# Paged keys and values: indirect loads of four tokens to a partition from Pool, weights moved to the sync queue

## The chip, the cores and the metric

The kernel runs on one core of one Trainium2 chip. The metric is the device time of one execution in microseconds (us), as the median of several runs. All arithmetic is float32.

## The reference, cut to what matters

One decoder layer handles 256 prompt tokens and 8 sample tokens (one for each of 8 sequences with 2048 past tokens). Sample attention is the part the change touches:

```python
past_k = cache_sb_k[layer][page_table].reshape(8, 16 * 128, 8, 64)   # 16 pages of 128 tokens a sequence
z = einsum(q, k) / 8 + bias                      # stick-breaking scores, no softmax
log_rest = log_sigmoid(-z)
log_stick = cumsum(log_rest, reverse=True) - log_rest    # over all later keys
a = exp(log_sigmoid(z) + log_stick);  out = einsum(a, v)
```

Around it stand: six modulation vectors from `w_ada`, one q/k/v projection, the same stick-breaking attention and a dilated softmax attention for the prompt, dilated attention of the samples over a 2048-token window (whose cache is also an output, shifted by one token), an output projection, and a PEER layer: top-16 of 16384 experts for each token and head, whose rows of 8 KB are gathered and weighted.

## The kernel before, in words

Each engine has its own program, and semaphores order them. All 48 weight chunks of 1 MB (line 378, a round is 4 chunks) are loaded by Pool's queue into four slots `R[0..3]`: rounds 0 and 1 are modulation, 2 to 4 q/k/v, 5 to 8 modulation again, 9 output projection, 10 and 11 the expert queries. A chunk's load waits until the tensor engine has used the one four before it (`w_used`).

The sync engine (SP) loads small inputs, then the K pages (line 285), each a direct DMA of 256 KB whose page number it reads into a register. A chunk is two pages (tokens on the partitions) in one of four slots; 64 chunks make up K, and 64 make up V. It waits for `k_used` or `v_used` of the chunk four before. SP also issues the copies of the window caches to the outputs (line 296): 64 pieces of 1 MB from HBM to HBM, in `copy_piece`. A piece waits for the landing of the previous piece on its own of four semaphores, so up to four are in flight. The order on SP is: 24 pieces early, then all K chunks, ten stores of new keys and values (lines 322 and 324), V chunks with some pieces between, the DV windows, and the remaining pieces.

VectorE (DVE) multiplies every K chunk by the query (line 1140) and reduces it over each head (line 1142), in `page_scores`. Sequences 0 to 3 are handled beside the q/k/v projection. Sequences 4 to 7 are threaded into four rounds of prompt attention, `sticks_pair(g)` on TensorE (PE): DVE's part of such a round is, in order, a scale (L1158), two chunks, L1164 and L1166, two chunks, L1170, two chunks, L1174, two chunks, a copy (L1177). PE computes two modulation chunks (L472) before and two after its own matmul in the round.

Pool applies the rotary factors (L395 to L399) once q/k/v is ready, stores two rows (L402, L403) and goes on with the weights. When K is done, DVE, ScalarE (ACT) and PE turn the scores into sticks: DVE sums over later pages in 15 steps (L1240), PE does the sum over tokens (L649, L650), DVE subtracts (L1246). Then `dilated_pair` on PE alternates V matmuls (`pages_pv`, L594: one matmul a page, in halves of 8 pages) with dilated prompt attention. Pool meanwhile fetches windows of the dilated K cache (L261, L262), which DVE consumes (L1221, L1223). After that come DV windows (L699), the output projection and queries (L510, L744), and the expert stream: Pool gathers 1 MB per slot by indirect DMA (L432), DVE dots it (L1454), PE accumulates (L791).

Of the kernel before, what the change touches and what calls it, by code (L numbers as in the profile page):

```python
# [35 lines left out]
KVP = 2  # L36
KVS = 4
CPB = NPG // KVP
# [20 lines left out]
for _name, _n in (("ident", P), ("tri", P), ("ones", P), ("later", P), ("cnt", 384), ("dbias", 384),  # L59
                  ("scnt", 384), ("sbias", 384), ("rope", 48), ("hmask", DG), ("unit8", 64), ("rep8", P), ("fold8", NB), ("iota", TOPK)):  # L60
    _CONST[_name] = (_at, _n)
    _at += _n
# [3 lines left out]
def constants():  # L66
# [36 lines left out]
    put("fold8", np.tile(np.eye(NB, dtype=np.float32), (2 * NH, 1)))  # L103
    put("iota", np.tile(np.arange(TOPK, dtype=np.float32), (P, 1)))
# [20 lines left out]
def build(nc, A):  # L125
    ctx = ExitStack()
    with ctx:
# [9 lines left out]
        def cst(name):  # L137
# [15 lines left out]
        zrow = sb("zrow", [NB * NH, 384])  # L153
# [5 lines left out]
        pages = sb("pages", [1, NB * NPG], I32)  # L159
# [12 lines left out]
        diag = sb("diag", [P, 4, P])  # L172

# [3 lines left out]
        KV = [Rf[:, WSLOTS * 2048 + s * 1024:WSLOTS * 2048 + (s + 1) * 1024].rearrange("p (g n) -> p g n", g=KVP)  # L177
              for s in range(KVS)]

# [6 lines left out]
        z1, zt, zl = Z[:, 0, :], Z[:, 1, :], Z[:, 2, :]  # L186

# [16 lines left out]
        def row_slot(k):  # L204
# [25 lines left out]
          kst dst sbs dis tks subk_in z_v topsm tope fin_in""".split()  # L230
# [36 lines left out]
        def _(sp):  # L267
# [12 lines left out]
            def page_chunk(b, c, cache, ready, waits):  # L280
                for sm, v in waits:
                    sp.wait_ge(sm, v)
                for g in range(KVP):
                    page = sp.value_load(pages[0:1, bass.ds(b * NPG + c * KVP + g, 1)], min_val=0, max_val=cache.shape[0] - 1)  # L284
                    sp.dma_start(KV[c % KVS][:, g, :],  # L285
                                 cache[bass.ds(page, 1)].rearrange("a p n -> (a p) n")).then_inc(ready[c % KVS], 16)
# [20 lines left out]
            for c in range(CPB):  # L307
                page_chunk(0, c, A["sb_k"], k_ready, [(s["k_used"], c - KVS + 1)] if c >= KVS else [])
                if c == KVS - 1:
                    copy_windows(0, 0)  # L310
                    copy_windows(0, 1)
                    copy_windows(1, 0)

            with sp.Fori(1, NB) as b:
                for c in range(CPB):
                    page_chunk(b, c, A["sb_k"], k_ready, [(s["k_used"], b * CPB + (c - KVS + 1))])


# [7 lines left out]
            def value_pages(b, first=False, q=None):  # L326
                for c in range(CPB):
                    page_chunk(b, c, A["sb_v"], v_ready,
                               [] if first and c < KVS else [(s["v_used"], b * CPB + (c - KVS + 1))])
                    if q is not None and c % 4 == 1:  # L330
                        copy_piece(2, 0, c // 4, q)


            for m in range(2):
                copy_piece(1, 1, m, 0)
            sp.wait_ge(s["k_used"], NB * CPB)
            value_pages(0, first=True, q=0)
            with sp.Fori(1, NB // 2) as i:
                value_pages(i * 2 - 1)
                value_pages(i * 2, q=i)  # L340
            value_pages(NB - 1)

# [26 lines left out]
        def _(pool):  # L369
            for k in range(WSLOTS):  # L370
                pool.dma_start(R[:, k, :], A["wts"][k]).then_inc(w_ready[k], 16)

            def weight_rounds(first, end):
                with pool.Fori(first, end) as r:
                    for k in range(WSLOTS):

                        pool.wait_ge(s["w_used"], r * WSLOTS + (k - WSLOTS + 1))
                        pool.dma_start(R[:, k, :], A["wts"][bass.ds(r * WSLOTS + k, 1)].rearrange("a p n -> (a p) n")  # L378
                                       ).then_inc(w_ready[k], 16)

            weight_rounds(1, 6)
# [22 lines left out]
            weight_rounds(6, 9)  # L404
# [6 lines left out]
            weight_rounds(9, 10)  # L411
            with pool.Fori(1, NB // 2) as i:
                for j in range(2):
                    pool.wait_ge(s["dk_used"], i * 2 + (j - 1))
                    window_rows(pool, DK, i * 2 + j, j, A["dil_k"], A["dil_k_s"], dk_ready)
# [1132 lines left out]
```

## Time and profile before

| | before |
|---|---|
| median of 3 runs | 1369.17 us (1368.55 to 1369.77) |
| profiled execution, first to last instruction | 1367.5 us |
| TensorE busy | 1121.9 us, 82% |
| VectorE busy | 790.2 us, 58% |
| ScalarE busy | 374.5 us, 27% |
| GpSimd busy | 389.7 us, 28% |
| moved by DMA | 479.79 MB, mean 351 GB/s |
| DMA queue of Pool | 332.47 MB |
| DMA queue of SP | 146.92 MB |

The profile gives no separate end-to-end time for its own execution; its span is 1.7 us below the median of the timed runs. Busy times overlap each other, so the shares say which engine could bound a stage, and only the order of the waits in that stage says which one does.

### The profile page before, as it was taken

The numbers are of one execution on the slowest core, as the hardware profiler recorded it, in microseconds if no ns is written. First come the engines' busy times: TensorE is split into PE (matmuls) and PEld (weight loads), VectorE is DVE, ScalarE is ACT, GpSimd is POOL, SyncE is SP. The second block draws the span as 40 slices with busy tenths as digits, with TensorE's granted clock in tenths as the row PEclk, the third lists the DMA queues.
The fourth block names the chain that finished last, engine by engine and source line by source line (L and its number), as shares of the span: only waits on it lengthen the run. The fifth ranks groups of instructions, "written<-read, shape, count | busy, mean of one in ns | idle before, by whom it ended". The sixth has DMA issues, their size and how long they took to land.

```text
span 1367.5 us, 14726 instructions
## 1 busy us (share of the span) xinstructions
PE 1121.9 (82%) x3386; PEld 503.3 (37%) x3386; DVE 790.2 (58%) x1679; ACT 374.5 (27%) x1030; POOL 389.7 (28%) x384
## 2 busy tenths in 40 slices
PE   6799998998787888998997778777768777777875
PEld 2375774443221211457852323233223333232321
DVE  4203996976512411324437777777777677777755
ACT  1201004434110000002233333333344334444323
POOL 1000003020201000000125555555535555555540
PEclk9898999996999997998999999999999999999998
DMA  9998887898698886899659999999999999999995
GB/s 335 426 358 303 298 312 270 323 356 301 220 284 252 251 269 215 322 390 339 232 207 423 422 422 422 422 422 422 422 421 379 422 422 422 422 422 422 422 422 221
DMA packets 91422, 479.79 MB, mean 351 GB/s; under 512 B 11792, under 2 KB 11817, under 8 KB 50172
## 3 DMA queue, kind: packets, MB, share of 16 engines
q0 software_dynamic: 46912, 332.47, 60.3%
q1 hardware_dynamic: 44476, 146.92, 30.9%
q8 instruction: 15, 0.25, 0.1%
q14 instruction: 19, 0.16, 0.0%
HBM read 476.10 MB, written 70.32 MB: 400 GB/s over the span
## 4 chain that ended last, share of the span: by engine, by line
PE 37%; DMA 32%; issue 10%; DVE 8%; SPq 6%; ACT 4%; POOL 2%; POOLq 0%; DVEq 0%; ACTq 0%
DMA R<-in_uv,idst 26%; PE ps L510 13%; PE ps L791 8%; PE ps L744 4%; SPq L284 3%; DMA R<-in_sb_v 3%; PE ps L472 3%; SPq L285 2%; DVE R L1140 2%; PE ps L699 2%; PE ps L594 2%; POOL R L432 2%; DMA R<-in_sb_k 2%; PE ps L481 1%; ACT wgt L1050 1%
## 5 line engine op out<-in xcount | busy, mean ns | idle before, releaser
L791 PE MATMUL ps<-R,diag 128*128 128x512 f32 x1024 | 482.1, 619 | 153.4 <-ACT diag L1069 153.4
L432 POOL DMA_INDIRECT R<-in_uv,idst x256 | 320.9, 1254 | 332.5 <-PE ps L791 260.4
L1454 DVE CUSTOM_DVE_ANT_0 R<-R,H 128x1024 f32<-128x1024 f32 x264 | 318.6, 1222 | 162.7 <-DMA R<-in_uv,idst 152.3
L791 PEld LDWEIGHTS ps<-R,diag 128*128 128x128 f32 x1024 | 192.4, 196 | 443.1 <-ACT diag L1069 241.6
L510 PE MATMUL ps<-R,HT 128*128 128x256 f32 (+1 forms) x768 | 172.7, 384 | 1.0 <-DVE HT L1335 0.4
L378 POOL DMA_DIRECT2D R<-in_wts x44 | 23.4, 531 | 508.9 <-PE ps L510 341.9
L594 PE MATMUL ps<-R,ast 128*8 128x512 f32 x256 | 123.0, 625 | 27.6 <-DMA R<-in_sb_v 24.0
L510 PEld LDWEIGHTS ps<-R,HT 128*128 128x128 f32 (+1 forms) x768 | 119.0, 158 | 55.3 <-issue 12.1
L1047 ACT ACTIVATE gel<-dots 128x2 f32<-128x2 f32 x132 | 26.8, 203 | 377.3 <-DVE dots L1454 377.3
L1140 DVE TENSOR_TENSOR R<-R 128x1024 f32<-128x1024 f32 x64 | 78.2, 1221 | 66.2 <-ACT R L874 57.6
L472 PE MATMUL ps<-R,cT 128*9 128x256 f32 x384 | 92.8, 398 | 1.3 <-ACT bsel L821 1.3
L1069 ACT ACTIVATE diag<-const,wgt 128x128 f32<-128x128 f32 x256 | 89.1, 394 | 16.1 <-PE ps L791 3.2
L1142 DVE TENSOR_REDUCE Z<-R 128x1024 f32 x64 | 78.1, 1220 | 9.1 <-DVE R L1140 0.2
L1258 DVE TENSOR_TENSOR msk<-ps,const 8x512 f32<-8x512 f32 x16 | 10.9, 679 | 97.4 <-PE ps L594 57.5
L594 PEld LDWEIGHTS ps<-R,ast 128*8 128x8 f32 x256 | 20.8, 92 | 119.6 <-issue 67.9
L1050 ACT ACTIVATE wgt<-gel,gst 128x1 f32<-128x1 f32 x264 | 63.3, 287 | 4.3
L744 PE MATMUL ps<-HT,R 128*128 128x264 f32 x256 | 59.9, 393 | 0.3 <-ACT HT L855 0.3
L472 PEld LDWEIGHTS ps<-R,cT 128*9 128x9 f32 x384 | 34.3, 94 | 55.8 <-issue 14.8
L744 PEld LDWEIGHTS ps<-HT,R 128*128 128x128 f32 x256 | 49.0, 194 | 8.6 <-ACT HT L855 0.4
L863 ACT ACTIVATE QKV<-ps 128x512 f32 (+1 forms) x12 | 7.2, 598 | 120.9 <-PE ps L510 120.9
L261 POOL DMA_DIRECT2D m_all<-in_dil_k x24 | 12.9, 538 | 95.6 <-DVE zd L1223 95.0
L699 PE MATMUL ps<-R,ast 128*8 128x512 f32 (+2 forms) x48 | 29.8, 775 | 7.9 <-DMA R<-out_dil_v_s 5.8
(233 smaller groups left out, 872.3 us busy)
## 6 DMA issues: line engine op xcount, KB each, us to landing
R<-in_wts POOLq DMA_DIRECT2D x48, 1024.0 KB, 8.1
R<-in_sb_k SPq DMA_DIRECT2D x128, 256.0 KB, 4.4
R<-in_sb_v SPq DMA_DIRECT2D x128, 256.0 KB, 3.4
out_dil_k_s<-in_dil_k SPq DMA_DIRECT2D x32, 1023.5 KB, 8.0
out_dil_v_s<-in_dil_v SPq DMA_DIRECT2D x32, 1023.5 KB, 7.9
R<-in_uv,idst POOLq DMA_INDIRECT x256, 12.1
m_all<-in_dil_k POOLq DMA_DIRECT2D x16, 192.0 KB, 6.1
R<-in_dil_v SPq DMA_DIRECT2D x16, 192.0 KB
```

The lines of the kernel that those rows point to most:

```text
L432: pool.indirect_dma_start(out=R[:, row_slot(k), :], out_offset=None, in_=A["uv"], in_offset=bass.IndirectOffsetOnAxis(ap=idst[:, par, k:k ...
L472: last = pe.matmul(out, cT[:, c, :], W[k][:, c, :], start=(c == 0), stop=False)
L510: last = pe.matmul(out, hT[:, c, t * P:t * P + TP[t]], W[k][:, c, :], start=(c == 0), stop=(c == KC - 1))
L594: last = pe.matmul(ps[0:NH, 6 + j, :], ast[:, j, c * KVP + g, :], KV[c % KVS][:, g, :], start=(c + g == 0), stop=(c * KVP + g == NPG - 1))
L699: last = pe.matmul(ps[0:NH, 6 + j, :], ast[0:n, j, g, :], DV[j][0:n, g, :], start=(g == 0), stop=(g == 2))
L744: last = pe.matmul(ps[:, j, 0:NTOK], W[k][:, c, j * P:(j + 1) * P], hT[:, c, :], start=(c == 0), stop=(c == KC - 1))
L791: last = pe.matmul(ps[:, banks + q, :], diag[:, k % 4, :], R[:, row_slot(k), D + q * 512:D + (q + 1) * 512], start=False, stop=False, skip ...
L1050: last = act.activation(wgt[:, k + q:k + q + 1], gel[:, k + q:k + q + 1], ACT.Copy, scale=gst[:, k + q:k + q + 1])
L1069: act.activation(diag[:, k % 4, :], ident, ACT.Copy, scale=wgt[:, k:k + 1]).then_inc(s["diag_done"], 1)
L1140: kc.inc(dve.tensor_tensor(kv, kv, q, ALU.mult))
L1142: dve.tensor_reduce(z4[:, c * KVP:(c + 1) * KVP, bass.ds(b, 1), :].rearrange("p g a h -> p g (a h)"), kv.rearrange("p g (h d) -> p g h d", ...
L1454: dve.tensor_tensor_reduce(u, u, H[:, t, :], 1.0, 0.0, ALU.mult, ALU.add, dots[:, k:k + 1]).then_inc(s["dot_done"], 1)
```

## The change

K and V pages are read through one view of the cache in which a row is 4 tokens (8 KB). A chunk is now four pages (1 MB): each partition gets four consecutive tokens of one page, 32 partitions to a page. There are 32 K and 32 V chunks, in two slots of 1 MB in place of four of 0.5 MB. Row numbers are computed once by DVE from the page table. Pool issues the chunks, one indirect DMA each, in program order with rotary work and windows. The weights move to SP, each followed by a copy piece in rounds 1 to 4 and 6 to 8. The sum over later keys is regrouped to fit the new token order.

```diff
-KVP = 2
-KVS = 4
-CPB = NPG // KVP
+QUAD = 32
+QUADS = P // QUAD
+KVT = P // QUAD
+KVS = 2
+CPB = NPG // KVT
+KVN = NB * CPB
@@ sync
-            sp.dma_start(pages[:, :], A["pages"]).then_inc(s["small_in"], 16)
-            sp.wait_ge(s["small_in"], 64)
+            for q in range(QUADS):
+                sp.dma_start(pages[q * QUAD:(q + 1) * QUAD, :], A["pages"][q:q + 1].to_broadcast([QUAD, KVN])).then_inc(s["pages_in"], 16)
+            for k in range(WSLOTS):
+                sp.dma_start(R[:, k, :], A["wts"][k]).then_inc(w_ready[k], 16)
+            def weight(r, k):
+                sp.wait_ge(s["w_used"], r * WSLOTS + (k - WSLOTS + 1))
+                sp.dma_start(R[:, k, :], A["wts"][bass.ds(r * WSLOTS + k, 1)].rearrange("a p n -> (a p) n")
+                             ).then_inc(w_ready[k], 16)
...
+            for k in range(WSLOTS):
+                weight(1, k)
+                copy_piece(0, k // 2, k % 2, 0)
+            with sp.Fori(2, 5) as r:
+                for k in range(WSLOTS):
+                    weight(r, k)
+                    copy_piece(0, k // 2, k % 2, r - 1)
+            for k in range(WSLOTS):
+                weight(5, k)
             sp.wait_ge(s["rot_done"], 6)
...
+            for k in range(WSLOTS):
+                copy_piece(1, k // 2, k % 2, 0)
+            with sp.Fori(6, 9) as r:
+                for k in range(WSLOTS):
+                    weight(r, k)
+                    copy_piece(1, k // 2, k % 2, r - 5)
+            for k in range(WSLOTS):
+                weight(9, k)
+            for q in range(4):
+                for k in range(WSLOTS):
+                    copy_piece(2, k // 2, k % 2, q)
             sp.wait_ge(s["new_out"], 32)
             sp.wait_ge(s["dk_used"], NB)
...
-                    copy_piece(1, 1, j, i)
-            sp.wait_ge(s["v_used"], NB * CPB)
+                    copy_piece(3, 0, j, i - 1)
+            sp.wait_ge(s["v_used"], KVN)
             sp.dma_start(subk, A["subk"].rearrange("p (g n) -> p g n", g=16)).then_inc(s["subk_in"], 16)
-            for pair, odd in ((2, 1), (3, 0), (3, 1)):
-                copy_windows(pair, odd)
+            with sp.Fori(10, 12) as r:
+                for k in range(WSLOTS):
+                    weight(r, k)
+            for m in range(2):
+                copy_piece(3, 0, m, 3)
+            copy_windows(3, 1)
@@ gpsimd
+            def page_rows(n, cache, ready, used):
+                if used is not None:
+                    pool.wait_ge(*used)
+                pool.indirect_dma_start(
+                    out=R[:, WSLOTS + n % KVS, :], out_offset=None, in_=cache,
+                    in_offset=bass.IndirectOffsetOnAxis(ap=pages[:, n:n + 1], axis=0),
+                ).then_inc(ready[n % KVS], 16)
+            pool.wait_ge(s["rows_ready"], 1)
+            for n in range(KVN // 2):
+                page_rows(n, A["sb_k"], k_ready, (s["k_used"], n - KVS + 1) if n >= KVS else None)
             pool.wait_ge(s["qkv_ev"], QKV_CH)
...
-            weight_rounds(6, 9)
+            for n in range(KVN // 2, KVN):
+                page_rows(n, A["sb_k"], k_ready, (s["k_used"], n - KVS + 1))
...
+            for i in range(NB // 2):
+                for n in range(i * 2 * CPB, (i + 1) * 2 * CPB):
+                    page_rows(n, A["sb_v"], v_ready, (s["v_used"], n - KVS + 1) if n >= KVS else (s["k_used"], KVN))
+                    if i < NB // 2 - 1 and n % CPB == 1:
+                        w = n // CPB + 2
+                        pool.wait_ge(s["dk_used"], w - 1)
+                        window_rows(pool, DK, w, w % 2, A["dil_k"], A["dil_k_s"], dk_ready)
@@ tensor
-            for half in range(2):
-                c = slice(half * 512, (half + 1) * 512)
-                pe.matmul(ps[:, 3 + half, :], tri, zl[:, c], start=True, stop=False)
-                last = pe.matmul(ps[:, 3 + half, :], ones, zt[:, c], start=False, stop=True)
+            n = CPB * PAIRS
+            pe.matmul(ps[:, 3, 0:n], tri, zt[:, 2 * n:3 * n], start=True, stop=False)
+            pe.matmul(ps[:, 3, 0:n], ones, zt[:, 3 * n:4 * n], start=False, stop=True).then_inc(s["z_s"], 1)
@@ vector: row numbers, page_scores on 128x2048 instead of 128x1024, the suffix sum
+            step(dve.tensor_scalar(rows_f[:, :], rows_f[:, :], float(QUAD), cst("place"), ALU.mult, ALU.add))
...
-                page_scores(g + 4, (0, 1))
+                page_scores(g + 4, (0,))
...
-            for g in range(NPG - 2, -1, -1):
+            step(dve.tensor_tensor(two, L[:, :, 0, :], L[:, :, 1, :], ALU.add))
+            step(dve.tensor_tensor(three, two, L[:, :, 2, :], ALU.add))
+            step(dve.tensor_tensor(total, three, L[:, :, 3, :], ALU.add))
```

## Rows read from the trace of the kernel before

**Rows 1.** Windows: stretch, its length, busy us by engine, PEclk, DMA share, GB/s.
```profile
0.00:123.50 123.50, 102.00 (x395) 53.54 (x396) 22.64 (x20) 21.20 (x48) 8.86 (x20) 0.90 0.96 370
123.50:215.40 91.90, 88.96 (x401) 61.03 (x400) 76.78 (x66) 9.90 (x22) 8.46 (x18) 0.98 0.85 286
215.40:320.00 104.60, 92.72 (x441) 44.91 (x441) 93.29 (x96) 37.85 (x70) 19.23 (x34) 0.89 0.91 326
346.40:512.80 166.40, 140.42 (x363) 30.52 (x363) 50.80 (x100) 14.29 (x39) 12.65 (x24) 0.95 0.84 262
560.00:705.80 145.80, 137.64 (x624) 102.28 (x624) 59.48 (x165) 27.85 (x82) 12.34 (x17) 0.94 0.80 296
705.80:1367.00 661.20, 497.02 (x1055) 194.72 (x1053) 466.81 (x1182) 245.35 (x729) 328.13 (x271) 0.97 0.98 408
```

**Rows 2.** DVE timeline, 123 to 323 us: start, duration, instruction, idle before it.
```profile
123.52 1.22 DVE L1140 TENSOR_TENSOR R<-R 128x1024 f32<-128x1024 f32 x1 [57.60 <-ACT R L874]
124.88 1.22 DVE L1142 TENSOR_REDUCE Z<-R 128x1024 f32 x1
126.01 1.22 DVE L1140 TENSOR_TENSOR R<-R 128x1024 f32<-128x1024 f32 x1
...
204.59 1.22 DVE L1142 TENSOR_REDUCE Z<-R 128x1024 f32 x1
214.35 1.14 DVE L1158 TENSOR_SCALAR H<-ps,sbb 128x384 f32<-128x384 f32 x2 [8.54 <-PE ps L554]
215.41 1.21 DVE L1140 TENSOR_TENSOR R<-R 128x1024 f32<-128x1024 f32 x1
...
240.48 1.13 DVE L1158 TENSOR_SCALAR H<-ps,sbb 128x384 f32<-128x384 f32 x2
...
289.63 1.14 DVE L1158 TENSOR_SCALAR H<-ps,sbb 128x384 f32<-128x384 f32 x2
...
319.95 1.22 DVE L1230 SCALAR_TENSOR_TENSOR Z<-Z,sbb 128x1024 f32<-128x1024 f32 x1
```

**Rows 3.** Waits, 215 to 320 us: DVE's on K pages.
```profile
DVE R L1140 <- DMA R<-in_sb_k: 6.5, 4, 3.2
```

**Rows 4.** POOL timeline, 210 to 223 us.
```profile
210.96 1.69 POOL L395 TENSOR_TENSOR Z<-QKV,const 128x128 f32<-128x128 f32 x4
...
221.32 0.59 POOL L402 DMA_DIRECT2D out_dil_k_s<-QKV  x1 [0.29 <-POOL QKV L399]
221.90 0.51 POOL L403 DMA_DIRECT2D out_dil_v_s<-QKV  x1
```

**Rows 5.** SP timeline: first and last of the ten stores.
```profile
310.78 1.24 SPq L322 DMA_DIRECT2D out_sb_k_p<-QKV  x2
...
317.33 0.97 SPq L324 DMA_DIRECT2D out_sb_v_n<-QKV  x1
```

**Rows 6.** DMA issues at 676, 189, 79, 587 and 635 us, last column us to landing.
```profile
R<-in_uv,idst POOLq DMA_INDIRECT x1, 5.6
...
R<-in_wts POOLq DMA_DIRECT2D x1, 1024.0 KB, 6.0
...
R<-in_wts POOLq DMA_DIRECT2D x1, 1024.0 KB, 13.3
...
R<-in_wts POOLq DMA_DIRECT2D x1, 1024.0 KB, 15.8
...
R<-in_wts POOLq DMA_DIRECT2D x1, 1024.0 KB, 10.8
```

**Rows 7.** PE timeline, 337 to 513 us.
```profile
337.50 1.92 PE L649 MATMUL ps<-Z,const 128*128 128x512 f32 x2
...
342.02 1.02 PE L650 MATMUL ps<-Z,const 128*128 128x512 f32 x2
...
346.36 7.03 PE L594 MATMUL ps<-R,ast 128*8 128x512 f32 x16 [1.59 <-ACT HT L887]
...
512.79 1.98 PE L481 MATMUL ps<-m_rows,const 9*128 9x512 f32 x4
```

**Rows 8.** Waits, 345 to 515 us: PE's on V pages and on ACT.
```profile
PE ps L594 <- DMA R<-in_sb_v: 24.0, 21, 3.6
PE ps L594 <- ACT HT L887: 3.4, 3, 1.6
```

**Rows 9.** SP timeline: the last copy piece.
```profile
643.30 0.51 SPq L296 DMA_DIRECT2D out_dil_v_s<-in_dil_v  x1
```

**Rows 10.** Timeline: Pool's first four weight loads, PE's first use of one.
```profile
1.41 2.32 POOL L371 DMA_DIRECT2D R<-in_wts  x4 [0.84 <-POOLq L1540]
...
14.13 5.09 PE L472 MATMUL ps<-R,cT 128*9 128x256 f32 x16 [0.60 <-ACT bsel L821]
```

More of the change, by code:

```diff
@@ L103, in constants @@
     put("fold8", np.tile(np.eye(NB, dtype=np.float32), (2 * NH, 1)))
+    put("place", (np.arange(P) % QUAD)[:, None].astype(np.float32))
     put("iota", np.tile(np.arange(TOPK, dtype=np.float32), (P, 1)))
@@ L158, in build @@
         gcol = sb("gcol", [P, KC])
-        pages = sb("pages", [1, NB * NPG], I32)
+        pages = sb("pages", [P, KVN], I32)
+        rows_f = sb("rows_f", [P, KVN])
         stat = sb("stat", [P, 32])
@@ L176, in build @@
         W = [R[:, s, :].rearrange("p (c n) -> p c n", c=KC) for s in range(WSLOTS)]
-        KV = [Rf[:, WSLOTS * 2048 + s * 1024:WSLOTS * 2048 + (s + 1) * 1024].rearrange("p (g n) -> p g n", g=KVP)
-              for s in range(KVS)]
+        KV = [R[:, WSLOTS + s, :].rearrange("p (g n) -> p g n", g=KVT) for s in range(KVS)]
         m_flat = m_all[:, :, :].rearrange("p s n -> p (s n)")
@@ L324, in _ @@
                 sp.dma_start(A[name], QKV[0:NB, 2, col:col + DG]).then_inc(s["kv_out"], 16)
[L326 to L341, printed above, removed]
+            for k in range(WSLOTS):
[9 more added lines that the diff above has]
+                    copy_piece(2, k // 2, k % 2, q)
             sp.wait_ge(s["new_out"], 32)
@@ L369, in _ @@
         def _(pool):
[L370 to L381, printed above, removed]
+            def page_rows(n, cache, ready, used):
[8 more added lines that the diff above has]
+                page_rows(n, A["sb_k"], k_ready, (s["k_used"], n - KVS + 1) if n >= KVS else None)
             pool.wait_ge(s["qkv_ev"], QKV_CH)
@@ L410, in _ @@
                 window_rows(pool, DK, b, b, A["dil_k"], A["dil_k_s"], dk_ready)
[L411 to L415, printed above, removed]
-            weight_rounds(10, CHUNKS // WSLOTS)
+            for i in range(NB // 2):
[5 more added lines that the diff above has]
+                        window_rows(pool, DK, w, w % 2, A["dil_k"], A["dil_k_s"], dk_ready)
             def head_rows(i, par, first):
@@ L590, in pages_pv @@
                     pe.wait_ge(s["ast_ready"], i + 1)
-                for c in range(half * 4, half * 4 + 4):
-                    pe.wait_ge(v_ready[c % KVS], (i * 2 + (c // KVS + 1)) * 32)
-                    for g in range(KVP):
-                        last = pe.matmul(ps[0:NH, 6 + j, :], ast[:, j, c * KVP + g, :], KV[c % KVS][:, g, :],
-                                         start=(c + g == 0), stop=(c * KVP + g == NPG - 1))
+                for c in range(half * 2, half * 2 + 2):
+                    pe.wait_ge(v_ready[c % KVS], (i * 2 + (c // KVS + 1)) * 16)
+                    for g in range(KVT):
+                        last = pe.matmul(ps[0:NH, 6 + j, :], ast[:, j, c * KVT + g, :], KV[c % KVS][:, g, :],
+                                         start=(c + g == 0), stop=(c * KVT + g == NPG - 1))
                     last.then_inc(s["v_used"], 1)
@@ L1117, in modulate @@
                     dve.tensor_tensor(H[0:n, t, :], H[0:n, t, :], b, ALU.add).then_inc(s["h_ready"], 1)
+            dve.wait_ge(s["pages_in"], 16 * QUADS)
+            dve.wait_ge(s["c_in"], 48)
+            step(dve.tensor_copy(rows_f[:, :], pages[:, :]))
+            step(dve.tensor_scalar(rows_f[:, :], rows_f[:, :], float(QUAD), cst("place"), ALU.mult, ALU.add))
+            dve.tensor_copy(pages[:, :], rows_f[:, :]).then_inc(s["rows_ready"], 1)
             dve.memset(m_all[:, 0:2, :], 0.0)
```

71 lines of the change are left out of this document (31 added, 40 removed).

## The prediction

> **What bounds the kernel now.** I read the windows by stage first, then the timeline of each engine in the stages that the change touches, then the waits there and the landing times of single DMAs. The windows [rows 1] give six stages. Up to 123.5 us and again from 560 to 705.8 us PE is the engine that runs through. From 123.5 to 215.4 us PE is busy 89.0 of 91.9 us with the q/k/v projection, and DVE does the first half of K beside it: its last reduce starts at 204.59 and it then idles 8.5 us for PE [rows 2]. From 215.4 to 320 us DVE is busy 93.3 of 104.6 us: this stage is DVE's. From 346.4 to 512.8 us PE is busy 140.4 of 166.4 us and waits 24.0 us for V pages [rows 1, 8]. From 705.8 us DMA moves 408 GB/s at a share of 0.98: the expert stream is bound by DMA, the change does not touch it, and it shifts as a whole with whatever comes before. So the change is decided between 123 and 513 us.
>
> The sums below are against the profiled execution, whose span is 1367.5 us; the median of the runs is 1.7 us above it, and I add the sum to the median.
>
> **The latency that decides: F.** With two slots of 1 MB, a chunk's load can start only when the chunk two before it is used. Call F the time from that point to usable data. A gather of the same shape (128 rows of 8 KB, from Pool) that ran alone landed 5.6 us after its issue [rows 6]; with 0.2 us for the wake-up F is 5.8. A Pool load of the same size beside SP's smaller page loads took 6.0. But Pool loads that ran while SP had up to four copy pieces in flight landed after 13.3, 15.8 and 10.8 us [rows 6]. The bounds are therefore 5.8 and 15.8. In the first four rounds of K after the change, SP's queue holds weights and copies in turn for most of the time, and I take F = 11 there, nearest to the lowest of the three contended rows because SP's queue also runs dry between its waits on `w_used`.
>
> By the Trainium skill (DMA: Bandwidth & Descriptors, Queues, rings and completion order) each DMA engine takes turns between the queues that have work, a packet at a time. By that rule the time would be that of the faster rival's upper end, 1364 us, and by the rows it is the sum below. The rows of 10.8 to 15.8 us do not agree with even turns.
>
> **First half of K (123.5 to 215.4).** A pair of 0.5 MB chunks costs 2 x (126.01 - 123.52) = 4.98 us of DVE now [rows 2]. One instruction over 2048 elements instead of two over 1024 saves its start: the gap of 1.36 us to the reduce and 1.13 us to the next chunk hold about 0.36 us that isn't proportional in all, so I take 4.6 us for 1 MB. Both slots are filled long before. Then two chunks cost F + 4.6. SP issues one weight and one piece in every 10.7 us here, which is about half the load of the contended rows: F about 8, between 5.8 and 11. Fourteen chunks after the first two: 7 x (8 + 4.6) + 9.2 = 97 us, so DVE ends near 221 instead of 206. DVE isn't needed before 215.4, and what follows waits for something later anyway (next step), so I cost it at nothing. If F were 11 this half would end at 242 and add some 8 us; that is kept for the range.
>
> **Chunk 16 comes late.** Now SP has the fifth sequence's chunks in place and DVE starts on them at 215.41. After the change the seventeenth chunk is behind Pool's rotary work in program order: that runs from 210.96 and its two stores end at 222.4 [rows 4]. The chunk is issued at 222.6 and is there at 233.6. At the same moment SP, released by the same rotary work, puts out ten stores (7.5 us of issuing [rows 5], 2.1 MB) and four copy pieces.
>
> **Second half of K (215.4 to 320).** Per round DVE has, beside four chunks, about 4.6 us of its own work in between (1.6, 0.9, 0.7 and 1.4). First round at F = 11: chunk 16 from 234 to 238.6, chunk 17 from 240.3 to 244.9, chunk 18 (issued 238.8) from 249.8 to 254.4, chunk 19 (issued 245.1) from 256.1 to 260.7, next round at 261.1. Before it was 240.48 [rows 2]: +20.6 us. Second and third round have four weights and four pieces each on SP: 2 x (11 + 4.6) = 31.2 us a round, against (289.63 - 240.48) / 2 = 24.6 [rows 2]: +13.2. In the fourth round SP has only the four weights of the output projection, F about 7.5: 24.2 us against 30.3 (in which 5.6 of the 6.5 us of DVE's waits for K now lie [rows 3]): -6.1. The end of K moves by 20.6 + 13.2 - 6.1 = +27.7 us. At F = 5.8 throughout, the same count gives 250.4 for the first round, then 23.1 us a round, bound by DVE: K ends at 319.7, +-0. At F = 15.8 it is +60.
>
> **Sticks (320 to 346.4).** The 15 adds are replaced by a shorter chain, but PE gets to the triangular product only at 337.5, long after they end, so they are worth nothing. The product takes 337.50 to 343.04 [rows 7] for eight records of 512 columns; four of 256 columns should take a quarter: -4 us. Bounds 0 and -5.5.
>
> **V (346.4 to 512.8).** Four chunks of 0.5 MB take PE 7.03 us [rows 7], so 1 MB takes 3.5. A half of `pages_pv` is two new chunks; there are 16 halves, 10.4 us each today. After the change each takes the larger of 7.03 + what PE has in between (about 1.3) and F + 3.5 = 9.3 at F = 5.8. SP's 16 pieces of the third pair start about 10 us before K ends and need at least 16.8 MB / 0.4 = 42 us, so they reach some 10 us into V: one half at 11 + 3.5 = 14.5. The first half has its data already (8.4), fourteen take 9.3, and the 3.4 us of waits on ACT stay [rows 8]: 8.4 + 130.2 + 14.5 + 3.4 = 156.5 against 166.4: -10 us. At F = 11 for six halves it would be +16; with no wait at all, 136 us, -30. Pool's window loads (2.2 us each) stand behind a V chunk and before the next trigger, which comes 3.5 us or more later, so they are hidden, except the first, which waits for DVE: within the 14.5.
>
> **The rest.** The first weights are issued by SP behind the small loads, near 8 us instead of 1.41; PE starts on them at 14.13 us [rows 10], when 2.6 MB of small loads and the first weight have passed at 370 GB/s [rows 1]: nothing, at most +2. The last ten pieces now wait behind the last weight at about 660 us, where before the last was issued at 643.30 [rows 9]. They share 10.5 MB with the first eight gathers; 18.9 MB fit into the 46 us to 705.8 at 408 GB/s, barely: +1.5 us, between 0 and +6. PE's weights for the second round of the K stage lie behind the stores and four pieces: 7.3 MB from 223 us, at the 290 GB/s which SP has when Pool takes a share, land at 248, and PE wants them at 261. They are covered by DVE's own lateness; without that lateness they would cost up to 8 us.
>
> **Sum.** +27.7 - 4 - 10 + 1.5 = +15.2 us; 1369.2 + 15.2 = 1384.4, rounded to 1385 us.
>
> **The rivals.**
> *Faster: K is not held up by SP's queue.* One mechanism: Pool's megabyte gets at least an even share. At the 408 GB/s of the expert stream 1 MB takes 2.6 us, so another megabyte beside it makes F = 5.8 + 2.6 = 8.4, and F is between 5.8 and that. For it: rows with SP's page loads in flight show 6.0; DMA has room, a share of 0.85 before 215 us [rows 1]. Against it: the rows of 13.3 and 15.8 [rows 6], and that 12 MB a round over the 23.1 us of DVE work would be 545 GB/s, above the 408 of the expert stream. At 8.4 K ends +10 (first round at 255, two of 26, one of 23.4), V -12, sticks -4, tail +1: 1364. At 5.8: 0 - 4 - 15 = 1350. The middle is 1357. The sign turns near F = 9. Chance 0.30.
> *No change.* F near 9, both cancel: 1367 to 1372. Chance 0.08.
> *PE starves for weights.* SP, one program, waits for a piece to land before it may issue the next weight; with Pool's queue busy, pieces land after 15 us and PE waits 8 us in each of three rounds on top of the forecast: 1385 + 24 = 1409. For it: weight and piece alternate on one queue; against: PE needs a weight only some 20 us after its slot comes free. Chance 0.09.
> *The page load is no better for being in rows of 8 KB*, F is above 11 in V too: +16 instead of -10 in V, so 1411. Only bandwidth sharing could do this and the copies end early. Chance 0.03.
>
> **How the numbers follow.** The forecast, F near 11 where SP's queue is full, has 0.50: 1385 us, with its own range 1374 to 1402. What a measurement of this kernel can tell from no change is 0.2%, 2.7 us. Faster 0.30; same 0.08; slower 0.50 + 0.09 + 0.03 = 0.62. The range that leaves out 2 in 10 runs from 1352, near the low end of the faster rival, to 1406.
>
> **What would show it.** Right: in the changed profile the first page product of the second half of K starts at 230 us or later instead of 215.4, after Pool's rotary work; single K loads between 222 and 300 us land after 9 us or more; DVE's waits for K grow from 6.5 to over 25 us in that stage; in V the halves are 9.3 us apart and PE's wait for V persists. Wrong: K loads landing in under 8 us beside SP's copies; PE waiting for weights on the critical chain; V longer than 166 us; or the expert stream changing its own length of 661 us by more than 3.

## The result and the profile after

| | before | after |
|---|---|---|
| median of 4 runs | 1369.47 us (1368.55 to 1374.68) | 1441.81 us (1438.16 to 1448.38) |
| ratio to before, 95% interval | | 1.0524 (1.0489 to 1.0559) |
| span of the profiled execution | 1367.5 us | 1446.6 us |
| first page product of K's second half | 215.41 | 236.78 |
| end of K (first L1230, now L1243) | 319.95 | 367.73 |
| PE ready for V; end of V | 346.4; 512.8 | 388.8; 593.2 |

The change makes the kernel 5.2% slower: the direction was forecast, but the size was 72 us instead of 16, outside the range. The spans differ by 79.1 us (the profiled execution of after was the longest of its four, at 1448.38 us). By stage that is +47.8 to the end of K, -5.3 in the sticks (21.1 against 26.4 us), +38.0 in V (204.4 against 166.4) and -1.4 in the rest.

Windows by stage of after, with the columns of [rows 1]:

```profile
0.00:125.40 125.40, 103.14 (x395) 54.87 (x396) 23.27 (x24) 21.24 (x48) 2.24 (x6) 0.90 0.68 273
125.40:226.40 101.00, 95.38 (x431) 63.05 (x429) 72.93 (x33) 9.92 (x22) 31.42 (x31) 0.99 0.72 270
226.40:367.70 141.30, 93.59 (x412) 47.70 (x412) 90.57 (x65) 38.33 (x70) 23.65 (x28) 0.76 0.95 371
388.80:593.20 204.40, 148.20 (x362) 32.43 (x362) 52.60 (x103) 15.92 (x43) 45.11 (x54) 0.87 0.70 239
640.00:783.00 143.00, 134.69 (x607) 99.83 (x606) 54.57 (x153) 28.08 (x83) 8.68 (x10) 0.95 0.50 185
783.00:1446.00 663.00, 505.19 (x1052) 198.17 (x1050) 470.14 (x1190) 245.77 (x729) 327.62 (x270) 0.95 0.98 409
```

DVE does no more work in the third row than before (90.6 against 93.3 us, [rows 1]); the row is 37 us longer because DVE waits. DMA's share was 0.85 in K's first half and is 0.72 now, and from 640 to 783 us it is 0.50, where in the matching stage before it was 0.80. So there was room for the copies, but not where SP now puts them.

DVE timeline of after, answering [rows 2] (start, duration, instruction, idle before it):

```profile
125.36 2.29 DVE L1153 TENSOR_TENSOR R<-R 128x2048 f32<-128x2048 f32 x1 [59.26 <-ACT R L881]
...
226.35 1.13 DVE L1171 TENSOR_SCALAR H<-ps,sbb 128x384 f32<-128x384 f32 x2
236.78 2.29 DVE L1153 TENSOR_TENSOR R<-R 128x2048 f32<-128x2048 f32 x1 [9.30 <-DMA R<-in_sb_k,pages]
...
259.12 2.29 DVE L1153 TENSOR_TENSOR R<-R 128x2048 f32<-128x2048 f32 x1 [10.05 <-DMA R<-in_sb_k,pages]
...
270.84 1.13 DVE L1171 TENSOR_SCALAR H<-ps,sbb 128x384 f32<-128x384 f32 x2
...
367.73 1.28 DVE L1243 SCALAR_TENSOR_TENSOR Z<-Z,sbb 128x1024 f32<-128x1024 f32 x1
```

POOL timeline of after, answering [rows 4]: the rotary work starts 6 us later than before, because a page load stands ahead of it, and chunk 16 stands behind it.

```profile
213.89 2.93 POOL L381 DMA_INDIRECT R<-in_sb_k,pages  x1 [4.76 <-DVE Z L1155]
216.93 1.69 POOL L402 TENSOR_TENSOR Z<-QKV,const 128x128 f32<-128x128 f32 x4
...
228.74 1.02 POOL L381 DMA_INDIRECT R<-in_sb_k,pages  x1 [0.30 <-issue]
```

Waits of after: DVE's on K pages from 226 to 368 us (6.5 us in [rows 3]), then PE's on V pages from 388 to 595 us (24.0 us in [rows 8]).

```profile
DVE R L1153 <- DMA R<-in_sb_k,pages: 47.5, 11, 10.1
...
PE ps L603 <- DMA R<-in_sb_v,pages: 56.1, 18, 12.9
```

PE timeline of after, answering [rows 7]. The triangular product is over at 387.1. The second V record below is one chunk, 8 matmuls, 18 us after the first.

```profile
385.37 1.06 PE L657 MATMUL ps<-Z,const 128*128 128x256 f32 x2
386.22 0.84 PE L658 MATMUL ps<-Z,const 128*128 128x256 f32 x2
...
396.91 5.29 PE L603 MATMUL ps<-R,ast 128*8 128x512 f32 x8 [8.12 <-DMA R<-in_sb_v,pages]
415.06 6.46 PE L603 MATMUL ps<-R,ast 128*8 128x512 f32 x8 [12.86 <-DMA R<-in_sb_v,pages]
...
433.30 2.73 PE L603 MATMUL ps<-R,ast 128*8 128x512 f32 x3 [10.91 <-DMA R<-in_sb_v,pages]
```

DMA issues of after at 242.2, 248.4, 367.8, 369.1 and 402.5 us, answering [rows 6] (last column: us to landing). All five are beyond my upper bound of 15.8.

```profile
R<-in_sb_k,pages POOLq DMA_INDIRECT x1, 16.9
...
R<-in_sb_k,pages POOLq DMA_INDIRECT x1, 17.4
...
R<-in_sb_v,pages POOLq DMA_INDIRECT x1, 29.0
...
R<-in_sb_v,pages POOLq DMA_INDIRECT x1, 45.9
...
R<-in_sb_v,pages POOLq DMA_INDIRECT x1, 30.8
```

SP timeline of after: the first of the ten stores and of the copies in K [rows 5], then the first and the last of the 16 pieces put out before V, and the last piece before the query weights [rows 9].

```profile
227.03 0.82 SPq L331 DMA_DIRECT2D out_sb_k_p<-QKV  x2
...
233.97 0.56 SPq L307 DMA_DIRECT2D out_dil_k_s<-in_dil_k  x1
...
363.02 0.54 SPq L307 DMA_DIRECT2D out_dil_k_s<-in_dil_k  x1
...
415.30 0.51 SPq L307 DMA_DIRECT2D out_dil_v_s<-in_dil_v  x1
...
627.31 0.54 SPq L307 DMA_DIRECT2D out_dil_v_s<-in_dil_v  x1
```

PE's first use of a weight comes at 15.79 us instead of 14.13 [rows 10].

### The profile page after: what moved, and what is told of

It reads as the page before. It is cut to its first block, busy times and chain, and to the rows that moved or that the text cites. A ratio compares the mean times of both kernels' runs of the same rounds, so it can differ in the third digit from the quotient of the medians.

```text
span 1446.6 us, 12757 instructions
## 1 busy us (share of the span) xinstructions
PE 1136.9 (79%) x3382; PEld 512.0 (35%) x3382; DVE 784.5 (54%) x1612; ACT 375.7 (26%) x1030; POOL 440.7 (30%) x400
## 4 chain that ended last, share of the span: by engine, by line
DMA 43%; PE 31%; DVE 10%; issue 8%; POOL 3%; ACT 3%; SPq 1%; POOLq 0%; DVEq 0%; ACTq 0%
DMA R<-in_uv,idst 22%; DMA R<-in_sb_k,pages 9%; DMA R<-in_sb_v,pages 9%; PE ps L798 8%; PE ps L519 6%; PE ps L603 6%; PE ps L751 4%; DVE R L1153 3%; DVE Z L1155 2%; POOL R L441 2%; PE ps L481 2%; DVE R L1473 2%; PE ps L706 1%; PE ps L490 1%; DMA R<-in_uv,idec 1%
## 5 line engine op out<-in xcount | busy, mean ns | idle before, releaser
L798 PE MATMUL ps<-R,diag 128*128 128x512 f32 x1024 | 491.4, 630 | 147.1 <-ACT diag L1076 147.1
L798 PEld LDWEIGHTS ps<-R,diag 128*128 128x128 f32 x1024 | 196.4, 199 | 442.2 <-ACT diag L1076 230.3
L603 PE MATMUL ps<-R,ast 128*8 128x512 f32 x256 | 130.4, 663 | 56.2 <-DMA R<-in_sb_v,pages 56.1
L1153 DVE TENSOR_TENSOR R<-R 128x2048 f32<-128x2048 f32 x32 | 73.4, 2294 | 132.6 <-DMA R<-in_sb_k,pages 73.2
L381 POOL DMA_INDIRECT R<-in_sb_k,pages x32 | 42.0, 1313 | 303.0 <-DVE Z L1155 287.8
L481 PE MATMUL ps<-R,cT 128*9 128x256 f32 x384 | 96.4, 409 | 2.3 <-DMA R<-in_wts 2.3
L381 POOL DMA_INDIRECT R<-in_sb_v,pages x32 | 34.0, 1064 | 152.6 <-PE ps L603 146.0
L1155 DVE TENSOR_REDUCE Z<-R 128x2048 f32 x32 | 73.2, 2286 | 5.3 <-DVE R L1153 1.5
L1277 DVE TENSOR_TENSOR msk<-ps,const 8x512 f32<-8x512 f32 x16 | 10.9, 678 | 99.2 <-PE ps L603 62.7
L1057 ACT ACTIVATE wgt<-gel,gst 128x1 f32<-128x1 f32 x264 | 63.5, 288 | 4.3
L429 POOL COPY idst<-idx 128x16 int32 (+1 forms) x16 | 7.2, 447 | 146.6 <-DVE gall L1463 146.6
```

The lines of the kernel that those rows point to most:

```text
L381: pool.indirect_dma_start(out=R[:, WSLOTS + n % KVS, :], out_offset=None, in_=cache, in_offset=bass.IndirectOffsetOnAxis(ap=pages[:, n:n + ...
L481: last = pe.matmul(out, cT[:, c, :], W[k][:, c, :], start=(c == 0), stop=False)
L603: last = pe.matmul(ps[0:NH, 6 + j, :], ast[:, j, c * KVT + g, :], KV[c % KVS][:, g, :], start=(c + g == 0), stop=(c * KVT + g == NPG - 1))
L798: last = pe.matmul(ps[:, banks + q, :], diag[:, k % 4, :], R[:, row_slot(k), D + q * 512:D + (q + 1) * 512], start=False, stop=False, skip ...
L1057: last = act.activation(wgt[:, k + q:k + q + 1], gel[:, k + q:k + q + 1], ACT.Copy, scale=gst[:, k + q:k + q + 1])
L1153: kc.inc(dve.tensor_tensor(kv, kv, q, ALU.mult))
```

## Experiments

All ratios are to the kernel before, on the same chip, with 95% intervals; medians of different kernels were in part taken on different chips, on which the kernel before took 1368.9 to 1370.3 us. The stages come from one execution of each kernel. In the diffs `pieces(n)` puts out the next n of the 64 copy pieces in their fixed order. Stages of each profile, in us (V from the start of the second triangular matmul record to the end of the last page product; waits of DVE for K pages and of PE for V pages in the whole kernel):

| kernel | K ends | V | waits K | waits V | ratio |
|---|---|---|---|---|---|
| before | 319.95 | 170.8 | 8.5 | 24.0 | 1 |
| after | 367.73 | 207.0 | 73.2 | 56.1 | 1.0524 |
| no copies | 341.35 | 171.2 | 47.2 | 27.6 | 0.9999 |
| copies out of V | 362.21 | 173.2 | 68.2 | 26.2 | 1.0285 |
| copies out of K | 338.57 | 199.3 | 44.1 | 51.3 | 1.0336 |
| both | 340.85 | 175.6 | 46.6 | 28.4 | 1.0140 |
| rotary later | 370.93 | 200.6 | 67.4 | 55.5 | 1.0547 |
| one piece in flight | 361.21 | 195.9 | 52.4 | 42.0 | 1.0516 |
| half slots, both | 329.85 | 150.0 | 25.9 | 9.7 | 0.9868 |
| half slots alone | 364.43 | 178.3 | 57.2 | 38.9 | 1.0373 |
| half slots, both, rotary later | 330.48 | 148.4 | 21.7 | 11.1 | 0.9889 |
| before, copies beside K | 343.27 | 170.2 | 32.1 | 26.1 | 1.0081 |
| both, query in PSUM | 338.26 | 167.3 | 45.0 | 23.3 | 1.0082 |

**No copies.** Theory: what costs is the copies on SP's queue beside Pool's loads.

```diff
 def pieces(n):
-    for _ in range(n): copy the next piece
+    pass
```

> All 64 copy pieces of the window caches are left out (two outputs are therefore not written except for the new row); everything else is as after the change. Theory A (Pool's page loads get a small share while SP's queue holds copy pieces): single page loads land in 5.5 to 8 us in every stage, K ends near 325 us instead of 368, V takes about 160 us instead of 204, the whole about 1355 us. Theory B (two slots and program order cost it, with or without copies): K still ends after 350 us and the whole stays above 1410 us. Theory C (indirect page loads are slow in themselves, or starved by DVE): landings stay above 9 us and the whole above 1420 us.

Measured: 1372.94 us, ratio 0.9999 (0.9971 to 1.0028). All of the loss is gone, but none of the gain that Theory A expected appears. K still ends 21.4 us later than before and V is as long as before. Some 8 us come back between the end of V and the first expert product (157 us instead of 165); the kernel before with copies beside K, which leaves no copy out, has 155 us there, so it is not shown that the spared copies save them. Windows of this kernel in K's second half and in V:

```profile
222.20:341.40 119.20, 91.90 (x437) 45.28 (x435) 90.36 (x66) 38.29 (x70) 25.71 (x34) 0.87 0.84 303
364.20:531.00 166.80, 139.17 (x363) 31.68 (x363) 51.59 (x100) 14.34 (x39) 44.84 (x54) 0.95 0.65 220
```

**Copies out of V only, and out of K only.** The 16 pieces before V go behind V in the first kernel; the 16 of K's second half go early, beside the q/k/v weights, in the second.

```diff
@@ first kernel
-            pieces(16)                       # before V
@@ after V: 4 pieces, then 2 with each of the eight last weights
@@ second kernel
-    weight(r, k); pieces(1)                  # r = 1 to 4, and 6 to 8
+    weight(r, k); pieces(1, 3, 3, 1 for r = 1 to 4), none from r = 5 on
-            pieces(4)                        # after the ten stores
```

> Only the 16 pieces that stood before V move to the stages after V. Theory A: the first two V loads land in under 9 us, not 29 and 46; V takes about 160 us; the whole drops by about 40 us, to 1400 us. Theory B: V shortens by under 10 us. In the later stages the pieces lie beside PE-bound work and cost 0 to 5 us.

Measured: 1409.96 us, ratio 1.0285 (1.0246 to 1.0325). V shrinks by 34 us, and PE's waits for V are back where they were before the change.

> Only the 16 pieces that lay beside the second half of K move ahead, before 125 us, where the copies ran in the kernel before. Theory A: K loads between 225 and 360 us land in 6 to 9 us instead of 8 to 17, K ends near 330 us, the whole drops by 35 to 40 us, to about 1405 us. Theory B: K ends no more than 12 us earlier, 1430 us.

Measured: 1415.2 us, ratio 1.0336 (1.0288 to 1.0384). K ends 29 us earlier, and V stays bad.

**Both.** Copies neither in K's second half nor before V.

> Both groups of 16 pieces are moved: 32 pieces ahead of 125 us, none beside the second half of K or beside V, the rest after V. If the two moves add up: 1442 - 32 - 27 = 1383 us. Theory A (copies in SP's queue starve Pool's page loads) then has accounted for nearly all of the loss, and K ends near 341 us as in the kernel without copies. Theory B (two slots and program order) owns what is left against 1370 us: the 21 us by which K still ends later.

Measured: 1386.52 us, ratio 1.014 (1.0096 to 1.0185). The two effects nearly add up: 2.4% and 1.9% of the 5.2%, 3.8% together. Its median is 14 us above that of the kernel without copies, while the spans of the two profiles differ by 2.8 us only. That is because the profiled execution of this kernel was the shortest of its four (1382.16 us, 4.4 below the median), and the one without copies was 6.4 above its median. So copies may still cost up to 14 us in the other stages, and the profiles don't place them.

**Rotary work behind two more page loads.** Rival to the queue: it is the program order on Pool that makes K late.

```diff
-            for n in range(KVN // 2):        # page loads ahead of the rotary work
+            for n in range(KVN // 2 + 2):
```

> Only Pool's order changes: chunks 16 and 17 of K are issued ahead of the rotary work. Theory A: DVE's 9.3 us wait for chunk 16 goes down to about 3, but the following loads meet SP's queue as before; -3 to -8 us, 1436 us. Theory B (program order is a main cause): -15 us or more.

Measured: 1448.77 us, ratio 1.0547 (1.0498 to 1.0596): no gain. The DVE timeline of this kernel shows chunk 16 on time, but the next two loads are then issued only at 244.3 and 245.6 us, behind the same rotary work: the wait for chunk 16 turns into one of 9.95 us for chunk 18.

```profile
228.09 1.13 DVE L1171 TENSOR_SCALAR H<-ps,sbb 128x384 f32<-128x384 f32 x2
229.13 2.34 DVE L1153 TENSOR_TENSOR R<-R 128x2048 f32<-128x2048 f32 x1
```

SP's stores, pieces and weights all wait for the rotary work too, so PE now runs out of weights in K's second half. PE's waits for them in the whole kernel (2.3 us in after):

```profile
PE ps L481 <- DMA R<-in_wts: 21.6, 6, 12.2
```

So this run moves the rotary work's lateness rather than removing it. It shows that two loads ahead of it gain nothing, not that the order on Pool is free.

**One piece in flight instead of four.** Is it the depth of SP's queue that holds Pool's loads up?

```diff
 def pieces(n):
     for each piece:
+        sp.wait_ge(landing of the piece before it)
         copy the piece
```

> The order of the changed kernel, but each copy piece waits for the landing of the piece issued before it, so one is in flight instead of four. If the depth of SP's queue sets Pool's share (Theory A): V loads at the start of V land in 9 to 12 us instead of 29 and 46, and V is shorter by 20 us or more, although the same bytes move beside it; the whole 1405 to 1420 us. If only the bytes count (rival): V is as long as before, 1435 us or more, and weights behind a piece come later.

Measured: 1439.12 us, ratio 1.0516 (1.046 to 1.0571). The V loads land sooner, the gain doesn't show: V is 11 us shorter, not 20. Queues of DMA in after from 376 to 415 us, beside four pieces (packets, MB, share of the engines' time):

```profile
q1 hardware_dynamic: 351, 11.46, 81.1%
q0 software_dynamic: 352, 2.22, 18.9%
```

The same of the kernel with one piece in flight, 391 to 440 us:

```profile
q1 hardware_dynamic: 239, 8.32, 45.7%
q0 software_dynamic: 1357, 8.21, 44.8%
```

With four pieces in SP's queue Pool gets 2.22 of 13.7 MB and its V loads land after 29 to 46 us; with one piece the two queues move about the same bytes and V loads land after 16 to 17 us at first, then 7.5 to 12. But SP's program now stops at each piece until the one before has landed, the weights behind it come late, and the copies beside V last until 477 us. Waits of the same kernel:

```profile
DVE R L1172 <- DMA R<-in_sb_k,pages: 52.4, 20, 10.6
PE ps L622 <- DMA R<-in_sb_v,pages: 42.0, 18, 5.2
...
PE ps L500 <- DMA R<-in_wts: 31.1, 9, 10.9
```

DVE and PE wait 35 us less for pages and PE 29 us more for weights (2.3 in after). That is my rival in which PE starves for weights; it holds in this kernel and, with 21.6 us, where the rotary work is later, but not in after.

**Four slots of 0.5 MB, copies moved.** What is left after the copies: with two slots, every second load starts only when a whole megabyte has been used. The same view in rows of two tokens (4 KB), four slots, still indirect from Pool.

```diff
-KVS = 2
+KVS = 4                                      # 0.5 MB each
-    out=R[:, WSLOTS + n % KVS, :], in_offset=rows pages[:, n]
+    out=R[:, WSLOTS + n % KVS // 2, half n % 2], in_offset=rows 2 * pages[:, n // 2] + n % 2
```

> As e7_all_pieces_moved, and each 1 MB chunk is loaded as two indirect DMAs of 0.5 MB (rows of 2 tokens, 4 KB) into four slots, each with a semaphore of its own, with 64 K and 64 V loads. Theory B (two slots are too few, since a load can't start before the chunk two before it is used): DVE waits for K drop from 47 to under 20 us, V from 166 to about 150 us, the whole to 1355 us or less, below the kernel before. Theory D (Pool issues each load late because it is held up while DVE runs on two SBUF inputs, 2.74 instead of 0.94 us): twice as many issues are held up and the whole is not better than e7.

Measured: 1353.13 us, ratio 0.9868 (0.9825 to 0.9911): 1.3% faster than the kernel before, and 2.7% faster than the same order of copies in slots of 1 MB. Windows of this kernel in K's second half and in V:

```profile
218.40:329.90 111.50, 89.11 (x429) 44.19 (x427) 93.79 (x98) 38.05 (x70) 51.62 (x50) 0.85 0.90 327
353.40:498.30 144.90, 133.36 (x362) 31.16 (x362) 51.33 (x100) 14.30 (x39) 72.44 (x84) 0.98 0.77 254
```

V is 21 us shorter than before [rows 1]; from the first round of K's second half to its end it is still 6 us longer (111.5 against 105.6).

**Four slots, copies where the change put them.**

> The half loads of e9 (four slots of 0.5 MB) with the pieces where the change put them. If depth and copies add up: 1442 - 33 = 1409 us. Theory A (starvation beside the copies in V doesn't depend on the slots): V begins late all the same, the first V loads take over 25 us, 1405 to 1420 us. Rival (half loads slip between the copies): below 1390 us.

Measured: 1419.91 us, ratio 1.0373 (1.0324 to 1.0422). It is 11 us above the 1409 of a plain sum. Half slots do not protect from the copies: the first four V loads land after 45.3 to 56.4 us. DMA queues of this kernel, 385 to 412 us:

```profile
q1 hardware_dynamic: 259, 8.52, 87.8%
q0 software_dynamic: 258, 0.94, 13.1%
```

**Four slots, copies moved, rotary work later.** The two edits above together.

> e9 with the first four loads of the second half of K issued ahead of the rotary work. In e9 DVE waits 10.5 us there. Theory (program order costs it once no copies are in the way): that wait falls to about 1 us, K ends 6 to 9 us earlier, 1345 us. Rival (the rotary work and the ten stores only move, and weights for the next round come later): within 2 us of e9, or slower.

Measured: 1353.13 us, ratio 0.9889 (0.9847 to 0.9932): the same as without the later rotary work. DVE's wait of 10.5 us at 230.0 becomes one of 8.0 us at 241.0, and K ends at 330.48 instead of 329.85. Putting the rotary work behind a few more loads gains nothing in either setting; what Pool's order costs as such stays untested.

**The kernel before, with copies beside K.** Would the old design be hurt by copies as well?

```diff
@@ kernel before, K chunks of sequences 4 to 7
+                    if c % 2:
+                        copy_piece(1, c // 4, c // 2 % 2, b - 4)
```

The same pieces leave the early batch and the V stage.

> The kernel before, with 16 pieces moved into SP's program beside the second half of K, one after every second chunk, as many as the changed kernel has there; pages still on SP, weights on Pool. Theory A in its general form (DMA is near its limit in that stage, and any copy there costs): K ends 20 to 35 us later, 1390 to 1400 us. Rival (only Pool's loads behind SP's copies suffer): K ends within 10 us, below 1380 us.

Measured: 1379.79 us, ratio 1.0081 (1.0053 to 1.0109). The whole ends between the two expectations, but K ends 23.3 us later (343.27 instead of 319.95), as Theory A in its general form has it: the same pieces cost the end of K 29.2 us in the changed kernel (367.73 - 338.57). So page loads on SP's own queue suffer from copies beside them nearly as much as Pool's do. The whole is only 10 us longer because 11 us come back between the end of V and the first expert product (155 us instead of 165). There the granted clock was 0.93 instead of 0.89 and PE was busy 144.1 instead of 151.3 us, and its waits for DV windows fell by 4.1 us; why the clock was higher is open. K pages of 256 KB take 9.4 us to land here (median, 240 to 300 us) and 4.9 in the kernel before in the same window.

**Scores with the query in PSUM.** See the last section for what it tests. Based on the kernel with both groups moved; the first four sequences' scores take another operand of the same shape.

```diff
-                    q = QB[:, b, :]          # SBUF
+                    q = ps[:, 4, :]          # PSUM, sequences 0 to 3
```

> e7 with the multiply of the first four sequences reading its second operand from PSUM in place of SBUF (the query there is not the right one, so the scores of these sequences are wrong; shapes and order are the same). Theory D (an indirect DMA on Pool is held up while DVE runs a tensor_tensor on two SBUF operands): in the first half of K all issues take 0.94 us, none 2.74; the waits of 3 us every second chunk fall to about 1.2, the first half ends 8 to 12 us earlier (near 214), the whole 3 to 8 us less than e7. Rival (2.74 us is Pool's own cost): the durations stay.

Measured: 1381.68 us, ratio 1.0082 (1.0056 to 1.0107), against 1.014 (1.0096 to 1.0185) without this edit; the intervals overlap, so a gain is not shown. The first half of K ends 2 us earlier, not 8 to 12, and the end of K 2.6 us. V differs by 8 us between the two profiles (167.3 and 175.6), though nothing in V was edited: differences of a few us between stages of single executions say little.

## Why the forecast had the right sign and the wrong size

**What held.** "Chunk 16 comes late": issued at 228.7 and first used at 236.8, forecast 222.6 and 233.6, by the mechanism named, though partly by luck: the issue was 6 us later than forecast and the landing, 7.9 us, 3 us shorter. The lone F, about: with no copies the first two V loads land after 8.2 and 9.3 us and the later ones after 5.4 to 8.6. Sticks: -5.3 against -4. The rest: -1.4 against +1.5, the expert stream 663 us against 661. The low chance of the rival in which PE starves: PE waits 2.3 us for weights in after. K loads between 222 and 300 us landed after 9.8 to 17.4 us but for the first one at 7.9, above the 9 that I named.

**The step that failed most: V, -10 forecast, +38.0 measured.** What failed is the price of the loads that meet the copies: I took F = 11 for one half and let the copies end 42 us after their start. In fact the four pieces in flight left Pool's queue 19% of the engines' time, loads landed after 29 to 46 us, and the 16 pieces were issued from 363.0 to 415.3 and so ended about 14 us (a piece's median landing) later, near 430: 67 us. PE's waits grew by 32.1 us and its busy time by 7.8 (148.2 against 140.4, at a mean clock of 0.87 against 0.95). Moving these pieces takes 34 us from V and 32 from the whole, which settles the cause. Nor was the number out of reach. I had read three contended rows; beside the early copies the trace of before holds a worse one, a weight load of Pool's issued at 49.14 us (DMA issues of the kernel before):

```profile
R<-in_wts POOLq DMA_DIRECT2D x1, 1024.0 KB, 28.0
```

(Part of it is a wait behind Pool's own previous load, which was issued at 44.33 and landed at 63.5.) A bound of 28 instead of 15.8 would have shown that the place of the pieces decides. My argument that the copies "end early" was the error: they were slow for the same reason that the pages were. The rival in which F is above 11 in V too, to which I gave 0.03, names what happened.

**The contended rows had half the depth.** I said that they ran while SP had "up to four copy pieces in flight". In the kernel before, the pieces of a window take turns on two of the four semaphores, so mostly two are in flight: 2.0 on average beside the load issued at 78.3 us, 2.4 beside the one at 587.3 and 2.0 beside the one at 634.6. The change goes round all four semaphores, so four are. That part of the change is not in my list of what it does. Landing of the pieces of one cache, before and after (last column, us):

```profile
out_dil_k_s<-in_dil_k SPq DMA_DIRECT2D x32, 1023.5 KB, 8.0
out_dil_k_s<-in_dil_k SPq DMA_DIRECT2D x32, 1023.5 KB, 14.6
```

With one piece in flight it is 7.1. No run has the change with two in flight and the pieces where it put them, so what the depth alone costs stays open: the run with one piece in flight has the late weights on top.

**K's second half, +27.7 forecast, +47.8 measured.** The forecast adds up the ends of the rounds. End of the first round: +20.6 forecast, +30.4 measured (270.84 instead of 240.48). About 3 us of the excess lie before chunk 16, which was first used at 236.78 instead of 233.6, and 6.6 after it: the next two loads, issued at 242.19 and 248.41, landed after 16.9 and 17.4 us and not after 11. Second and third rounds: +13.2 forecast, +21.1 measured (70.2 us instead of 49.2). They took 36.6 and 33.6 us, which the forecast's own 2 x (F + 4.6) gives at F = 13.7 and 12.2; single loads landed after 8.2 to 14.5 us. Fourth: -6.1 forecast, -3.7 measured (26.7 instead of 30.3). So the term that was mis-sized is again F beside the copies. The first half of K, which I put at nothing, ended at 226.4 and not at 221. DVE then still waited 9.3 us for chunk 16, so this lateness counted only by another way: Pool's rotary work is queued behind the last page load of the first half, which waits for DVE, so it moved from 210.96 to 216.93, and chunk 16 with it.

**Terms hidden under the first error.** With the copies gone K still ends 21.4 us late, where I forecast nothing at F = 5.8. Of these, 17.1 us are there at the end of the first round (257.60 instead of 240.48), after a wait of 11.6 us for chunk 16; this is the place where Pool's program order and the landing time work together, and no run takes them apart. Single loads land after 5.5 to 10.9 us even then, beside the weights on SP. Issues that DVE holds up (below) add little: without them K ends 2.6 us earlier. V without copies took 166.8 us, where the terms of the forecast at F = 5.8 give 8.4 + 15 x 9.3 + 3.4 = 151 us: its halves took 10.7 us on average (15 of them from 364.20 to 524.02), not 9.3. So about 15 of the 48 us by which V was missed are there without the copies. The same shows in after, where the halves from 539 us on took 10.4 to 12.4 us, with no copy left from that stage and no window load. Four slots take 11 us from the end of K and 26 us from V, against the same order of copies in two slots. That the slots and not the row size are the reason is likely but not isolated: rows shrank from 8 to 4 KB together with the chunks, so the runs show only that the longer rows bring nothing which outweighs the fewer slots.

**Even turns between queues.** By the Trainium skill (DMA: Bandwidth & Descriptors, Queues, rings and completion order) each engine takes turns among the queues that have work, one packet at a time. The prediction read this as even bytes, so that F is at most 8.4, and held its rows of 10.8 to 15.8 us against it. That reading was wrong. The fences above count 351 packets of SP's queue to 352 of Pool's beside four pieces, and 259 to 258 with half slots; the kernel with copies out of K only has 461 to 464 from 341 to 390 us. The turns are even, and the trace agrees with the page. What differs is the packet. In after, from 376 to 415 us, a copy piece is 16 packets of 65,504 bytes, which took 2.9 us each, and a row of a page is a packet of 8,192 bytes, which took 0.43 us; the other half of the packets of SP's queue have 4 bytes, one behind each copy packet, and I take them for the semaphore updates. So equal turns give 11.46 MB to 2.22 MB. From the shares in that fence, a turn of both queues took 1.44 + 0.34 us. If the 128 rows of a load are spread evenly over 16 engines, it needs eight turns and one for its update, 16 us by this estimate; the V loads of after landed at 396.8, 415.0 and 433.3, 18 us apart. Half slots have rows of 4 KB, so half the bytes need as many turns, which fits that they did not help beside the copies. With one piece in flight there are 239 packets to 1357: SP's queue is empty while the program waits for the landing, and the near-equal 45.7% and 44.8% are no sign of even turns. Copies in smaller packets would test this account; no run has them.

**Accounting of the 5.2%.** Copies before V 2.4%, copies in K 1.9% (each by the run that moves them alone), 3.8% together; 1.4% remains, and four slots turn it into -1.3%. What stays open: where the 14 us lie by which the kernel with both groups moved is above the one without copies, and what Pool's program order costs by itself. The change also moved page loads from SP to Pool and made them indirect, and no run takes these two back alone.

## What to carry to other kernels

Background copies belong where DMA has idle share and no one waits on a single load; here that was before K's second half and after V, and the place alone was worth 55 us (1441.8 - 1386.5). A load that is double-buffered with the latency on its path should never be priced by its lone landing time, nor by another kernel phase with a shallower queue beside it: read how many transfers the other queue will hold, and how long one of its packets takes. And when a change makes chunks bigger in the same memory, count the slots first: four slots of 0.5 MB, with rows half as long, beat two of 1 MB by 33 us here once the copies were out of the way.

## What the runs showed of the hardware that I had not expected

**Two busy queues get equal numbers of packets, not equal time.** Beside four copy pieces of 1 MB Pool's queue got 352 of 703 packets but 18.9% of the engines' time, and with rows of 4 KB 258 of 517 packets but 13.1%. Beside one piece, where SP's queue runs empty, it got 44.8%.

**DVE holds up Pool's indirect DMA.** Issuing an indirect page load takes Pool 0.94 us when DVE is reducing (0.94 to 1.02 when it is idle), and 2.74 us in four of the 14 issues of K's first half, 2.80 in a fifth, each triggered while DVE multiplies 128x2048 elements with two SBUF operands (2.29 us). Beside DVE's shorter steps in the second half it is 1.14 to 1.41 us. POOL timeline of the kernel with both groups moved, then of the one whose second operand is in PSUM:

```profile
130.37 2.74 POOL L397 DMA_INDIRECT R<-in_sb_k,pages  x1 [113.50 <-DVE Z L1171]
135.00 0.94 POOL L397 DMA_INDIRECT R<-in_sb_k,pages  x1 [1.89 <-DVE Z L1171]
143.75 2.74 POOL L397 DMA_INDIRECT R<-in_sb_k,pages  x1 [7.81 <-DVE Z L1171]
```

```profile
129.71 0.94 POOL L397 DMA_INDIRECT R<-in_sb_k,pages  x1 [113.36 <-DVE Z L1173]
134.34 0.94 POOL L397 DMA_INDIRECT R<-in_sb_k,pages  x1 [3.68 <-DVE Z L1173]
144.48 0.94 POOL L397 DMA_INDIRECT R<-in_sb_k,pages  x1 [9.21 <-DVE Z L1173]
```

All 14 issues of that stage take 0.94 us with the PSUM operand, so the second SBUF operand is the cause of the hold-up. What it costs the kernel is small: the next round starts at 224.21 instead of 226.25 us. The Trainium skill (SBUF — State Buffer, Who interferes with whom) says that a DVE instruction with two SBUF inputs contends with a GpSimd instruction that reads SBUF, and the trace agrees for the building of an indirect DMA. With half-size instructions (128x1024) the issue of a 0.5 MB load takes 1.67 us. Pool's direct DMAs, issued in the kernel before while such an instruction ran, took 0.50 to 0.56 us as at other times.
